# Layer 2's first gate tile moved ahead of the fourth group's queries, and half a weight tile lowered by VectorE

## The reference

```python
def diff_mixer(h, w_in, lq1, lk1, lq2, lk2, subln, w_out, lambda_init):
    proj = h @ w_in                       # 1024 -> 4096: q, k, v and gate, 1024 columns each
    q, k = rope(q, pos), rope(k, pos)     # 8 heads, two components of 64 each
    def block(args):                      # 128 queries at a time
        s = jnp.einsum('bqhcd,bkhcd->bchqk', qblk, k) * scale
        s = jnp.where(kpos[None, :] <= qpos[:, None], s, -jnp.inf)
        p = jax.nn.softmax(s, axis=-1)
        a = p[:, 0] - lam * p[:, 1]
        return jnp.einsum('bhqk,bkhd->bqhd', a, v)
    o = rmsnorm(o, subln) * (1.0 - lambda_init)
    y = o.reshape(B, S, DIFF_WIDTH) * jax.nn.silu(gate)
    return y @ w_out
```

## Time and profile before

| | |
|---|---|
| median of 3 runs | 2640.03 us (2639.12 to 2641.21) |
| the profiled execution | 2639.08 us, its span 2637.8 us |
| granted TensorE clock, mean | 0.999 |
| TensorE matmuls (PE) | 2607.4 us busy, 99% of the span, 13561 instructions |
| VectorE, ScalarE, GpSimd (DVE, ACT, POOL) | 47%, 39%, 44% |
| chain of work that ended last | PE 94%, DVE 3%, ACT 1%, POOL 1%, issue 1% |
| DMA | 282.22 MB, mean 107 GB/s |

### The profile page before, as it was taken

The page is one execution under the profiler, slowest core; times in us unless marked ns, Lnnn a source line. Parts: engine busy times, 40 slices in busy tenths (PEclk is TensorE's granted clock), DMA queues, the critical chain, the costliest instruction groups (busy, mean ns, idle before and its releaser), DMA issues.

```text
span 2637.8 us, 35473 instructions
## 1 busy us (share of the span) xinstructions
PE 2607.4 (99%) x13561; PEld 2120.3 (80%) x13561; DVE 1250.3 (47%) x2448; ACT 1038.0 (39%) x1939; POOL 1149.4 (44%) x890
## 2 busy tenths in 40 slices
PE   8999999999999999999999999999999999999998
PEld 6888878778778877777888888887777788888887
DVE  4535354553566365446155333365544624542426
ACT  4343434443546344453333424234445233342422
POOL 4434334435343354334464445454333346444443
PEclk9999999999999999999999999999999999999999
DMA  6434343333331333234442333333222435233331
GB/s 196 131 102 121 103 113 113 112 114 103 97 105 64 103 96 88 82 95 131 138 153 86 109 96 96 96 98 117 80 81 78 150 110 175 80 112 96 96 96 64
DMA packets 215121, 282.22 MB, mean 107 GB/s; under 512 B 22016, under 2 KB 155620, under 8 KB 214184
## 3 DMA queue, kind: packets, MB, share of 16 engines
q1 hardware_dynamic: 214952, 279.95, 34.5%
HBM read 246.28 MB, written 16.84 MB: 100 GB/s over the span
## 4 chain that ended last, share of the span: by engine, by line
PE 94%; DVE 3%; ACT 1%; POOL 1%; issue 1%; DMA 0%; ACTq 0%; DVEq 0%; POOLq 0%
PE banks L1808 37%; PE banks L1805 30%; PE banks L1801 13%; PE banks L1826 2%; PE banks L1940 1%; PE banks L1865 1%; PE banks L1922 1%; PE banks L2043 1%; PE banks L2070 1%; PE banks L1974 1%; PE banks L1908 1%; PE banks L2028 1%; PE banks L2056 1%; DVE AR L2553 1%; PE banks L1996 1%
## 5 line engine op out<-in xcount | busy, mean ns | idle before, releaser
L3179 POOL TENSOR_TENSOR WS<-WR,WS 128x512 fp32r<-128x512 f32 (+2 forms) x672 | 857.6, 1309 | 1015.8 <-ACT WS L2188 1015.8
L1808 PE MATMUL banks<-WS,UT 128*128 128x512 f32 (+1 forms) x3312 | 720.1, 370 | 3.1 <-DVE UT L2553 3.1
L1805 PE MATMUL banks<-UT,WS 128*128 128x512 f32 (+1 forms) x3024 | 707.4, 392 | 0.7 <-ACT AR L2377 0.7
L1805 PEld LDWEIGHTS banks<-UT,WS 128*128 128x128 f32 (+1 forms) x3024 | 561.9, 187 | 131.4 <-issue 14.7
L1808 PEld LDWEIGHTS banks<-WS,UT 128*128 128x128 f32 x3312 | 559.7, 188 | 113.8 <-issue 17.0
L2188 ACT ACTIVATE WS<-WR 128x1024 fp32r<-128x1024 f32 (+1 forms) x344 | 333.4, 1019 | 215.7 <-PE banks L1808 139.0
L1801 PE MATMUL banks<-UT,WS 128*128 128x512 f32 x1536 | 367.3, 394 | 0.0
L1801 PEld LDWEIGHTS banks<-UT,WS 128*128 128x128 f32 x1536 | 283.4, 188 | 64.4 <-issue 7.0
L1808 PE MATMUL banks<-WS,AT 128*128 128x512 f32 x1296 | 300.3, 390 | 0.9 <-ACT WS L2188 0.5
L1808 PEld LDWEIGHTS banks<-WS,AT 128*128 128x128 f32 x1296 | 242.4, 188 | 52.1 <-ACT WS L2188 1.3
L3177 POOL TENSOR_TENSOR WS<-WR,WS 128x512 fp32r<-128x512 f32 x128 | 182.2, 1455 | 226.4 <-ACT WS L2184 226.4
(11 more groups left out here) (225 smaller groups left out, 2534.0 us busy)
## 6 DMA issues: line engine op xcount, KB each, us to landing
WR<-in_w_in SPq DMA_DIRECT2D x112, 512.0 KB, 3.6
WR<-in_w_up SPq DMA_DIRECT2D x88, 512.0 KB, 3.5
WR<-in_dil_w_in SPq DMA_DIRECT2D x64, 512.0 KB, 3.7
WR<-in_w_down SPq DMA_DIRECT2D x40, 512.0 KB, 3.7
WR<-in_diff_w_in SPq DMA_DIRECT2D x32, 512.0 KB, 3.7
WR<-in_dil_w_in SPq DMA_DIRECT2D x32, 256.0 KB, 3.4
AR<-AF SPq DMA_DIRECT2D x128, 64.0 KB, 2.7
AR<-AF SPq DMA_DIRECT2D x64, 128.0 KB, 2.5
```

What stands on the lines that cost most here:

```text
L1805: mm = pe.matmul(B[bank][0:c, :], w[part][:, kk, g * P:g * P + c], act[:, other, kk, :], start=start, stop=stop)
L1808: mm = pe.matmul(B[bank][:, off:off + n], act[:, other, before_k + kk, g * P:g * P + P], w[part][:, kk, :], start=start, stop=stop)
L3179: ge.tensor_tensor(slot(i, 1)[:, s], raw(i)[:, s], slot(i, 0)[:, s].bitcast(F32), ALU.subtract).then_inc(lo_p.sem, 1)
```

## The change

The first gate tile of layer 2, l2g0, is loaded and made between k2 and q3, and the products of its two halves with the gate are kept for later (`early`). The generators yield 0 at the two places where the ratio changes: at 1.2 (`R_L2`) up to k2, at 0.85 (`R_L2B`) beside l2g0, then at 1.4 (`R_G2`) beside q3 and k3 and the other three gate tiles. The first chunk of each pair of layer 2 is put off by three ticks and not by four. Of tile l1o2 POOL lowers the first half; the second is lowered by DVE in a step of its own, `lo_half`, which stands ahead of layer 1's chunks 6 and 7, and after which SP loads the half of the tile after next.

```diff
-R0, R1, R2, R3, R_L1, R_L2, R_G1, R_G2 = 0.994, 1.0, 1.45, 0.54, 0.64, 1.2, 1.15, 1.7
+R0, R1, R2, R3, R_L1, R_L2, R_G1, R_G2 = 0.994, 1.0, 1.45, 0.54, 0.64, 1.2, 1.15, 1.4
+R_L2B = 0.85
...
+        if p == 3:
+            out.append(("l2g0", KC, 256, [(0, cols(w, 3072))]))
         for name, o in (("q", 0), ("k", 1024)):
...
-        return i > 0 and self.tiles[i][0][2:] != "d23" and self.tiles[i][0] != "l1o3"
+        return i > 0 and self.tiles[i][0][2:] != "d23" and self.tiles[i][0] != "l1o3" and (self.tiles[i][0], v) != ("l1o2", 1)
...
-            self.lows += [(i, v) for v in range(4)]
+            self.lows += [(i, v) for v in range(4) if self.by_pool(i, v // 2)]
...
-                    self.soon(4, lambda: self.step("chunk", name, 2 * j))
+                    self.soon(4 if name == "l1g" else 3, lambda: self.step("chunk", name, 2 * j))
...
-        for j in range(4):
+        for j in range(1 if early else 0, 4):
...
         self.fill(self.opened + 3)
+        self.step("lo_half", self.opened + 2, 1)
         for c in (6, 7):
             self.step("chunk", "l1g", c)
...
+            if p == 2:
+                yield 0
+            if p == 3:
+                yield from self.token_major("l2g0", first_gate)
+                yield 0
             while p >= 2 and p - 2 not in attended:
                 yield 1
...
+        def first_gate(i, half):
+            self.step("gate", i, half, 0)
+            early.append((i, half, 0))
...
-        self.beside(main(), att, R_L2)
-        self.beside(self.gates("l2g", lambda j: j in normed, late, set()), att, R_G2)
+        walk = main()
+        self.beside(itertools.takewhile(lambda t: t, walk), att, R_L2)
+        self.beside(itertools.takewhile(lambda t: t, walk), att, R_L2B)
+        self.beside(walk, att, R_G2)
+        self.beside(self.gates("l2g", lambda j: j in normed, late, set(), early), att, R_G2)
...
+                elif kind == "lo_half":
+                    i, v = a
+                    h = tiles[i][1] * tiles[i][2] // 2
+                    s = slice(v * h, v * h + h)
+                    ve.wait_ge(hi.sem, hi.at[i, v])
+                    tt(slot(i, 1)[:, s], raw(i)[:, s], slot(i, 0)[:, s].bitcast(F32),
+                       ALU.subtract).then_inc(lo_v.sem, 1)
```

More of the change, by code:

```diff
@@ L1 @@
+import itertools
 import math
@@ L120, in weight_tiles @@
             wide(f"l2v{p // 2}", w, 2048 + 256 * p)
+        if p == 3:
+            out.append(("l2g0", KC, 256, [(0, cols(w, 3072))]))
         for name, o in (("q", 0), ("k", 1024)):
             out.append((f"l2{name}{p}", KC, 256, [(0, cols(w, o + 256 * p))]))
-    for j in range(4):
+    for j in range(1, 4):
         out.append((f"l2g{j}", KC, 256, [(0, cols(w, 3072 + 256 * j))]))
@@ L307, in staged, with by_pool @@
                     yield from stages[s](i - s)
-    def by_pool(self, i):
-        return i > 0 and self.tiles[i][0][2:] != "d23" and self.tiles[i][0] != "l1o3"
+    def by_pool(self, i, v=0):
+        return i > 0 and self.tiles[i][0][2:] != "d23" and self.tiles[i][0] != "l1o3" and (self.tiles[i][0], v) != ("l1o2", 1)
     def split(self):
@@ L524, in program, with gates @@
             self.ffn(l)
-    def gates(self, name, done, late, gated):
+    def gates(self, name, done, late, gated, early=()):
         across = self.feature_major if name == "l1g" else self.token_major
-        waiting = []
+        waiting = list(early)
         def settle():
@@ L663, in layer2 @@
     def layer2(self):
-        projected, attended, normed = set(), set(), set()
+        projected, attended, normed, early = set(), set(), set(), []
         def project(p):
@@ L1217, in lo_done @@
         def lo_done(i, v=1):
-            return (lo_p.sem, lo_p.at[i, 2 * v + 1]) if order.by_pool(i) else (lo_v.sem, lo_v.at[i, v])
+            return (lo_p.sem, lo_p.at[i, 2 * v + 1]) if order.by_pool(i, v) else (lo_v.sem, lo_v.at[i, v])
         def is_end(l, which, b):
@@ L1270, in build @@
                         lo_v.plan((a[0], v))
+            elif kind == "lo_half":
+                lo_v.plan(tuple(a))
             elif kind == "lo":
@@ L2312, in scalar @@
                     if j > 0:
-                        se.wait_ge(timed.sem, timed.at[i - 1, half])
+                        se.wait_ge(timed.sem, timed.at[index[f"{tiles[i][0][:3]}{j - 1}"], half])
                     se.activation(fat(3072 + 512 * half, 512), B[gate_bank(i, half)][:, :], ACT.Tanh,
@@ L3246, in sync @@
                         load_half(i + 2, v)
+                elif kind == "lo_half":
+                    i, v = a
+                    sy.wait_ge(hi.sem, hi.at[i, v])
+                    sy.wait_ge(lo_v.sem, lo_v.at[i, v])
+                    load_half(i + 2, v)
                 elif kind == "lo" and a[1] % 2 == 1:
```

## The result

| | before | after |
|---|---|---|
| median | 2640.03 us | 2658.83 us (2658.55 to 2659.13, 5 runs) |
| ratio | | 1.0071, 95% interval 1.0061 to 1.0082 |
| span of the profiled execution | 2637.8 us | 2657.8 us |
| PE busy in it | 2607.4 us | 2614.4 us |
| granted TensorE clock, mean | 0.999 | 0.997 |

The change costs 18.8 us. The forecast was +8.8 us, range 2642.0 to 2652.5: the sign was right, the size was less than half, and the time lies 6.3 us above the range.

What follows compares the result with a forecast made beforehand. TensorE was taken as the bound, busy 99% with 7.16 us idle at the places changed. Terms -1.6 - 0.7 + 1.55 + 1.0 + 8.5 = +8.8 us gave 2648.8 us, range 2642 to 2652.5 (8 in 10).

Steps and rivals of the forecast that it cites:

- part one: End of layer 1: DVE lowering half of l1o2 removes PE's 1.84 us wait for POOL, adds 0.2; -1.6 us.
- small waits of layer 2: Layer 2: waits of 0.37, 0.15 and 0.21 us go, 0.65 before unit 18 returns behind q3's rotation; -0.7 us.
- end of the third group, units 22 and 23: In l2g1: transpose and product pairs stand next to each other without gate matmuls between, giving two waits; +1.55 us.
- beginning of l2g1, unit 22's transpose: Behind k3's last matmul: DVE's work before chunk 0 holds the corner bank unit 22's transpose needs; +1.0 us, range 0 to +3.
- end of layer 2, idle time: Behind the last gate matmul: the last units' chain leaves PE idle 9.4 us before chunk 6, against 0.83; +8.5 us.
- the rival's +2: Before chunk 6: PE's long gap halves the clock, losing 2 us and a little more; 2651 us, chance 0.17.
- No chunk but 0 is waited for: Layer 2: sooner chunks move each pair's first chunk up one half block, which doesn't reach the end's idle time.
- the drain costs half: End of layer 2: DVE and ACT overlap more, or thinner pacing removes small waits; +3 us, 2643, chance 0.24.
- faster: Layer 2 and layer 1's end: pacing clears 4.89 us of waits, part one saves 2.27; 2634 us, chance 0.05.

Runs made afterwards that it cites:

- third experiment: The changed kernel with chunks 0 and 1 of layer 2's gate put off by six more ticks; 2653.27 us, ratio 1.0051.
- fourth experiment: The changed kernel with the copies that spread k3 issued two ticks earlier, right behind its rotation; 2657.12 us, ratio 1.0066.
- tenth: The changed kernel with chunks 0 and 1 six ticks later and filler ratio 3.0 instead of 1.4 beside the last three gate tiles; 2650.89 us, ratio 1.0042.
- fifth: The kernel before with only the filler ratio R_G2 changed, 1.4 instead of 1.7; 2647.39 us, ratio 1.0028.
- sixth: The changed kernel with only the l2g0 move kept: ratios 1.7 and 1.2 as before, chunks from the fourth tick, no lo_half; 2654.21 us, ratio 1.0054.
- eighth: The changed kernel with chunks 0 and 1 six ticks later and filler ratio 2.0 instead of 1.4 beside the last three gate tiles; 2651.30 us, ratio 1.0042.
- twelfth: The changed kernel with l2g0 put back behind the fourth group's keys, all else kept; 2645.42 us, ratio 1.0020.
- second: The changed kernel with the first chunk of each pair put off by four ticks as before; 2654.23 us, ratio 1.0054.
- seventh: The changed kernel with unused matmuls added, 34 ahead of unit 22's transpose and 14 ahead of chunk 6; 2657.00 us, ratio 1.0064.
- first experiment: The kernel before with only the second half of l1o2 lowered by DVE, layer 2 untouched; 2637.54 us, ratio 0.9993.

## Why the prediction was wrong

| step of the prediction | forecast | measured |
|---|---|---|
| part one | -1.6 | -0.9 |
| small waits of layer 2 (0.65, 0.15, 0.21, 0.37 go; 1.17 at 837.61 is new) | -0.7 | -0.2 |
| end of the third group, units 22 and 23 | +1.55 | +1.4 |
| **beginning of l2g1, unit 22's transpose** | **+1.0** | **+7.6** |
| end of layer 2, idle time | +8.5 | +6.2 |
| clock behind unit 22 | 0 | +2.6 (to 2.9) |
| clock at the end (4.59 against 3.01 us) | 0, the rival's +2 | +1.6 |
| sum | +8.8 | +18.3, of 20.0 between the profiled executions (18.8 by the medians) |

The 1.7 us between this sum and the profiles are assigned to no place.

**The step that failed** is the third point of part two, the beginning of l2g1, which had the wait before unit 22's transpose at 1.0 us more; it measured 7.6. It reckoned with PE and DVE: who stands before chunk 0 in DVE's order, and when the corner bank comes free. It named 0 to +3 us, and for DVE's pile alone that range held (3.01 us in the third experiment, 1.9 over the 1.12 of before). But between PE's transpose and DVE's read of the bank stands ACT, and ACT's first chunk waits for the DMA copies of q3 and k3 (for k3's shown by the fourth experiment). In the profile before, that wait took no time and so had no row; it stood in the code, and its slack was some 14 us: the l2g0 tile that the change takes away. The step weighed the spread of k2, which moves ahead of the tile, and not that of k3, which comes right ahead of chunk 0 at the new seam.

**"No chunk but 0 is waited for"** was right and read the wrong way: it was said to put the chunks' new tick aside, and chunk 0 was the one that it moved. One tick of it was some 4 us.

**The clock** was given 0.17, at the end alone, at a price of 2 us. It fell at both places and cost some 4 (2.6 and 1.6). The Trainium skill (TensorE: Matmul & The Clock Gate, What's actually happening) says that the array falls back to its halved clock when idle; the traces agree, behind 3.01 us in the third experiment (805.08: 1.11 us for four transposes that take 0.60) and already behind 2.23 us in the tenth.

**The end of layer 2** was right in mechanism and in time: 16.9 against 17.9 us from the gate's last matmul to chunk 6. From the gate's last matmul to the norm's start it took 12.0 us (forecast 11.6), from there to chunk 6 4.9 (forecast 6.3, after the 6.7 of before): DVE's pairs for the norm and for the product with the gate took 1.29 us each (870.14 and 871.54), where they had taken 2.37 and 2.39 in the kernel before, beside POOL's low parts. PE's own work up to there came to 9.8 us and not 8.5, so 7.1 us were idle and not 9.4. The fifth and sixth experiments put one thing right: the term isn't owed to both causes together. The thinner filler with the tile in its old place loses 7.0 us there (4.3 idle, 2.7 by the clock), and the moved tile with the old ratio has the same 3.72 us and the same half speed.

**Part one** was mis-sized by its one price. The same form beside the same partner took 1.19 us before and 2.03 after; the range's other end (2.8 us, no gain) was as near as the value I took.

The two rivals that held 0.29 between them (the drain costs half, faster) need waits under those of before; nothing of the kind is to be seen.

## What to carry to other kernels

When a tile is moved forward, ask of everything that used to come behind it what it waited for without its showing: a wait that took no time in the old profile has no row, and its slack may be just the work that goes. Read the waits of all engines between the two ends of a bank's life in the code, DMA landings above all, and not only the queue of the engine that the profile names. And weigh a long gap of TensorE at more than its length: in layer 2 of these kernels every gap of 2.88 us or more was followed by matmuls at half speed, which cost 1.4 to 2.9 us more.

## What the runs showed of the hardware

- The clock fell behind waits of 8.75, 6.66, 4.44 (eighth and twelfth experiments), 3.72, 3.01, 2.88 (sixth) and 2.23 us (tenth). Behind one of 2.49 us (third, 870.80: 0.63 us for four transposes, then 3.00 for twelve matmuls) and one of 2.01 (eighth) it didn't. Often the first row behind the wait still has the full clock and the next has not (changed kernel: 0.63 us at 875.03, then 4.59). In the second, third and seventh experiments it fell without a long wait, among some of 0.7 to 0.9 us, and in the second one of 2.02 us, 8 us behind an earlier fall, had 1.93 us for eight matmuls behind it that take 1.16. What decides between these stays open.
- Dummy matmuls in the gap kept the clock up both times, at 802 to 810 (34 of them) and at 859 to 863 (14), and won 2.6 us by PE's rows and 2.0 us by the times.
- A DVE subtraction of 128x1024 with both inputs in SBUF took 1.19 us in one profile, 2.03 us in the other and 2.32 in the first experiment's, beside POOL's low parts each time; a POOL quarter beside it took 2.4, 2.0 and 1.5 us (1.25 with DVE mostly idle, changed kernel from 877.63: four in 5.02). Rotations of 128x512 took 0.65 and 1.2 to 1.5 us. So "beside POOL" has no single price, and either of the two can pay it.
- A step of DVE on 128x1 took 1.04 us instead of 0.22 beside POOL (802.22 and 811.01 in the changed kernel).
